# A decoder layer with 32 experts: the last expert pair's rows added by one-hot products on TensorE, and routing weights applied by diagonal products

## The reference

```
g_w, g_idx = top_k(softmax(xt @ w_rg + b_rg), 1)          # one group of 4
e_w, e_idx = top_k(softmax(e_logits of that group), 2)    # two experts of its 8
w = e_w / sum(e_w) * g_w
for e in range(32):
    h = silu(xt @ w_e_gate[e]) * (xt @ w_e_up[e])         # 1024 -> 256
    y = y + combine[:, e:e + 1] * (h @ w_e_down[e])       # 256 -> 1024
x = x + y;  out = rmsnorm(x, final_norm_g)
```

## Time and profile before

| | |
|---|---|
| median of 3 runs | 892.48 us (892.04 to 895.05) |
| the profiled execution's own time | 894.15 us |
| its span, first to last instruction | 892.4 us |
| PE, DVE, ACT, POOL busy | 89%, 42%, 24%, 9% of the span |
| expert weights | 96 transfers of 1 MB |
| mean granted clock of TensorE | 0.965 of full speed |

### The profile page before, as it was taken

The page is one execution under the profiler, slowest core; times in us unless marked ns, Lnnn a source line. Parts: engine busy times, 40 slices in busy tenths (PEclk is TensorE's granted clock), DMA queues, the critical chain, the costliest instruction groups (busy, mean ns, idle before and its releaser), DMA issues. The chain is left out here.

```text
span 892.4 us, 12013 instructions
## 1 busy us (share of the span) xinstructions
PE 795.0 (89%) x4643; PEld 583.0 (65%) x4643; DVE 371.0 (42%) x859; ACT 211.5 (24%) x388; POOL 77.1 (9%) x106
## 2 busy tenths in 40 slices
PE   5999999999999899999899999998999977787730
PEld 4887887779788666679899988987333322332210
DVE  2597566661700467348343347455111111101118
ACT  2320300001242334455343242120111100100003
POOL 0100230000111000000000000012111101001000
PEclk9999999999999999999999999997999999989975
DMA  9461283121446433310214344079999999999846
GB/s 365 158 203 48 72 90 105 52 90 55 172 164 215 166 112 126 142 49 1 95 60 166 142 176 157 25 295 386 380 418 419 420 422 421 419 421 421 338 115 262
DMA packets 33976, 186.09 MB, mean 209 GB/s; under 512 B 5915, under 2 KB 6187, under 8 KB 16808
## 3 DMA queue, kind: packets, MB, share of 16 engines
q1 hardware_dynamic: 21712, 146.63, 41.5%
q0 software_dynamic: 11344, 35.21, 12.4%
q10 hardware_dynamic: 864, 3.47, 1.0%
HBM read 176.14 MB, written 17.22 MB: 217 GB/s over the span
## 5 line engine op out<-in xcount | busy, mean ns | idle before, releaser
L479 PE MATMUL ps<-sb 128*128 128x288 f32 (+14 forms) x3038 | 595.3, 430 | 55.9 <-DMA sb<-in_wexp 32.4
L479 PEld LDWEIGHTS ps<-sb 128*128 128x128 f32 (+5 forms) x3038 | 388.2, 169 | 235.6 <-issue 149.1
L479 PE MATMUL ps<-sr 128*128 128x288 f32 (+1 forms) x1200 | 158.5, 292 | 1.2 <-DVE sr L1767 1.2
L479 PEld LDWEIGHTS ps<-sr 128*128 128x128 f32 x1200 | 155.1, 189 | 2.1 <-DVE sr L1767 1.4
L488 PEld LDWEIGHTS ps<-sb 128*128 128x128 f32 (+3 forms) x405 | 41.7, 140 | 35.4 <-issue 27.9
L2018 DVE SCALAR_TENSOR_TENSOR sb<-sb,ps 128x256 f32<-128x256 f32 x16 | 6.7, 421 | 125.2 <-ACT sb L1352 125.2
L488 PE MATMUL ps<-sb 128*128 128x128 f32 (+3 forms) x405 | 53.4, 270 | 4.9 <-DVEq L1846 2.0
L1767 DVE TENSOR_TENSOR sr<-sb,sr 128x2048 fp32r<-128x2048 f32 (+2 forms) x25 | 45.0, 1818 | 16.0 <-ACT sr L1239 12.8
L2026 DVE COPY sb<-ps 128x1024 f32<-128x1024 f32 x16 | 19.6, 1224 | 75.0 <-PE ps L479 75.0
L1057 ACT ACTIVATE sb<-ps 128x576 f32<-128x576 f32 (+4 forms) x29 | 22.9, 789 | 94.6 <-PE ps L479 66.9
L1755 DVE SCALAR_TENSOR_TENSOR sb<-sb,ps 128x576 f32<-128x576 f32 x24 | 18.0, 752 | 62.3 <-PE ps L479 62.3
(11 more groups left out here) (243 smaller groups left out, 435.8 us busy)
## 6 DMA issues: line engine op xcount, KB each, us to landing
sb<-in_wexp SPq DMA_DIRECT2D x96, 1024.0 KB, 28.8
sb<-in_wstream SPq DMA_DIRECT2D x34, 1024.0 KB, 5.0
sb<-in_mkT POOLq DMA_DIRECT2D x8, 512.0 KB, 7.3
sb<-in_mv POOLq DMA_DIRECT2D x8, 512.0 KB, 5.3
sb<-expert_rows SPq DMA_DIRECT2D x8, 512.0 KB, 9.3
sb<-in_xT ACTq DMA_DIRECT2D x4, 576.0 KB, 8.9
sb<-in_x SPq DMA_DIRECT2D x4, 512.0 KB, 7.3
sb<-k_pad POOLq DMA_DIRECT2D x8, 256.0 KB, 10.4
```

The lines of the kernel that those rows point to most:

```text
L479: return signed(nc.tensor.matmul(*a, **kw))
```

## The change

The diff also merges some semaphores of the first stages into one (`ones_set`, `zero_set`; `exp_ssm`, `trig`; `y_built`, `vt_built`), with the same points waited for. The rest is this:

- **The last pair isn't scattered.** `HELD` is pair 15. Its result stays in `M_YO` in SBUF. Instead of it, at the beginning of the expert stage, POOL scatters a tile of zeros to its rows of `expert_rows` (a memset of 128x1024, and one scatter after the gather of pair 2).
- **One-hot matrices.** In the expert stage, after pairs 9 to 13, DVE builds for each token tile (`hold`) a matrix that has a token's routing weight at the slot of pair 15 that holds it, and two diagonal matrices of the tile's weights w0 and w1. PE turns the one-hot matrices at pair 14 (`turn_held`, five transposes) and ACT copies them (`held_turned`, three copies).
- **The sum on PE.** At the end PE forms for each token tile, in PSUM, diag(w0) * y0 + diag(w1) * y1 + onehot * y15: three products for each half of 512 columns, six for each tile, 30 in all. DVE then adds PSUM to h in one operation.
- **Blocks of the last pair reordered.** `down(14)` stands ahead of `gate_up(15, 1)`, on PE and in the list of chunks, and `result(14)` ahead of `hidden(15)` on DVE.
- **Loads.** The five tiles of `expert_rows` go to ring slots that are free by then, and their loads wait for the scatters of pairs 0 to 14 and of the zeros. The load of the gain stands ahead of them in SP's order, and waits only for the turn of pair 15's rows.

```
@@ plan_chunks
-            chunks += [("gu", i, h, x) for h in range(2) for x in range(2)] if i < end else []
-            chunks += [("d", i - 1, 0, x) for x in range(2)] if i > first else []
+            halves = [[("gu", i, h, x) for x in range(2)] for h in range(2)] if i < end else [[], []]
+            before = [("d", i - 1, 0, x) for x in range(2)] if i > first else []
+            chunks += halves[0] + before + halves[1] if i == end - 1 else halves[0] + halves[1] + before
@@ SP
+            sp.wait_ge(xt_ps, NPAIR)
+            load_gain()
+            sp.wait_ge(ew_used, FIRST_Y + TT)
+            for s in range(2):
+                sp.wait_ge(y_sent[s], 16 * (NPAIR // 2))
+            load_results()
+
             with sp.If(overflow(sp) > 0):
...
-            for s in range(2):
-                sp.wait_ge(y_sent[s], 16 * (NPAIR // 2))
-            sp.dma_start(at(M_GF, (1, D)), bass.AP(rows.tensor, rows.offset + D, [[0, P], [1, D]])).then_inc(ld["gf"], 16)
-            for t in range(TT):
-                R = WROWS[t]
-                for k in range(2):
-                    sp.dma_start(at(A_WG + t * 2048 + k * D, (1, D), pn=R),
-                                 y_d[k * T + WTOK[t]:k * T + WTOK[t] + R, :]).then_inc(ld_row[t], 16)
@@ PE
+            def turn_held():
+
+                pe.wait_ge(pick_ready, 2 * TT)
+                pe.wait_ge(hT_sb, HELD - 1)
+                for t in range(TT):
+                    R = WROWS[t]
+                    last = turn_tile(pat(2, HELD_PS[t], (1, R)), at(R_SEL[t], (1, 128), pn=R), at(O_ID, (1, R), pn=R))
+                last.then_inc(held_ps, 1)
+
             def body(i, first, last):
                 gate_up(i, 0)
                 if not first:
                     turn_hidden(i - 1)
+                if last:
+                    down(i - 1)
                 gate_up(i, 1)
                 if not last:
                     turn_rows(i + 1)
-                if not first:
+                if i == HELD - 1:
+                    turn_held()
+                if not first and not last:
                     down(i - 1)
...
+            pe.wait_ge(held_sb, 1)
+            for t in range(TT):
+                R = WROWS[t]
+                if t == TT - 1:
+                    pe.wait_ge(y_sum, t - 3)
+                pe.wait_ge(ld_row[t], 48 if t < TT - 1 else 64)
+                for k in range(2):
+                    for half in range(2):
+                        mm(pat(t % 4, half * 512, (1, 512), pn=R), at(DIAG_AT[2 * t + k], (1, R), pn=R),
+                           at(Y_AT[t] + k * D + half * 512, (1, 512), pn=R), start=(k == 0), stop=False)
+                if t == 0:
+                    pe.wait_ge(y_copied, NPAIR)
+                for half in range(2):
+                    last = mm(pat(t % 4, half * 512, (1, 512), pn=R), at(R_SEL[t], (1, R)),
+                              at(M_YO + HELD % 2 * 1024 + half * 512, (1, 512)), start=False, stop=True)
+                last.then_inc(more_ps, 1)
@@ ACT
+            def held_turned():
+
+                act.wait_ge(held_ps, 1)
+                fn(at(R_SEL[1], (1, 384)), pat(2, HELD_PS[1], (1, 384)), ACT.Copy)
+                fn(at(R_SEL[4], (1, 128)), pat(2, HELD_PS[4], (1, 128)), ACT.Copy)
+                c.do(fn(at(R_SEL[0], (1, 64)), pat(2, HELD_PS[0], (1, 64)), ACT.Copy), held_sb)
@@ DVE
+            def hold(t):
...
+                for k in range(2):
+                    op(v.tensor_scalar(at(DIAG_AT[2 * t + k], (1, R), pn=R), at(O_ID, (1, R), pn=R),
+                                       at((R_W0, R_W1)[k] + t, (1, 1), pn=R), None, ALU.mult), False)
+                    op(v.tensor_tensor(at((R_SEL[t], tmp)[k], (RB, 2), (1, RB), pn=R), at(R_IOTA, (0, 2), (1, RB), pn=R),
+                                       at(R_RA + n5 * k + t, (0, 2), (0, RB), pn=R), ALU.is_equal))
+                    op(v.tensor_tensor(at((R_SEL[t], tmp)[k], (RB, 2), (1, RB), pn=R), at((R_SEL[t], tmp)[k], (RB, 2), (1, RB), pn=R),
+                                       at(R_HW + 2 * n5 * k + 2 * t, (1, 2), (0, RB), pn=R), ALU.mult))
+                c.do(v.tensor_tensor(at(R_SEL[t], (1, 128), pn=R), at(R_SEL[t], (1, 128), pn=R), at(tmp, (1, 128), pn=R), ALU.add),
+                     pick_ready)
...
             def pairs(i0, i1):
                 for i in range(i0, i1):
+                    if i == i1 - 1:
+                        result(i - 1)
                     hidden(i)
-                    if i > i0:
+                    if i0 < i < i1 - 1:
                         result(i - 1)
+                    if HELD - 6 <= i < HELD - 1:
+                        hold(i - HELD + 6)
                 result(i1 - 1)
...
-                dve.wait_ge(ld_row[t], 48 if t < TT - 1 else 64)
-                op(v.scalar_tensor_tensor(h, at(A_WG + t * 2048, (1, D), pn=R), at(R_W0 + t, (1, 1), pn=R), h, ALU.mult, ALU.add))
-                c.do(v.scalar_tensor_tensor(h, at(A_WG + t * 2048 + D, (1, D), pn=R), at(R_W1 + t, (1, 1), pn=R), h,
-                                            ALU.mult, ALU.add), y_sum)
+                dve.wait_ge(more_ps, t + 1)
+                c.do(v.tensor_tensor(h, h, pat(t % 4, 0, (1, D), pn=R), ALU.add), y_sum)
@@ POOL
+            nc.gpsimd.memset(at(M_YO + HELD % 2 * 1024, (1, 1024)), 0.0).then_inc(xg_clear, 1)
...
+                    if i == 0:
+                        scatter(HELD, zeros=True)
                     if i > i0:
                         scatter(i - 1)
-                scatter(i1 - 1)
```

More of the change, by code:

```diff
@@ L161 @@
 R_BV, R_CNT = R_LG, R_TM
+HELD = NPAIR - 1
+R_HW = R_GE
+HELD_PS = [768, 256, 384, 512, 640]
+DIAG_AT = [R_RH + 128 * j for j in range(4)] + [O_KTS + 128 * j for j in range(4)] + [M_WR + 128 * j for j in range(2)]
+FIRST_Y = CHUNK_AT["gu", HELD - 1, 0, 1] - 4
+Y_AT = [SLOTS_E[(FIRST_Y + t) % NSLOT] for t in range(TT)]
+M_TJ = SLOTS_E[(FIRST_Y + TT + 1) % NSLOT]
 assert 10 * OVER <= 40 * TT
-assert _at[0] <= O_Z
+assert _at[0] <= O_Z and O_KTS + 512 <= O_ID and M_WR + 256 <= M_BR
 def plan_jobs():
@@ L1017, in _ @@
             pairs(0, NPAIR)
-            with pe.If(overflow(pe) > 0):
+            flag = overflow(pe)
+            with pe.If(flag > 0):
                 pe.wait_ge(oh2_ready, 1)
@@ L1026, in _ @@
                 pairs(NPAIR, NPAIR_ALL)
+                pe.wait_ge(y_copied, NPAIR_ALL)
+                for t in range(TT):
+                    pe.wait_ge(ld_row[t], 80 if t < TT - 1 else 96)
+            pe.wait_ge(held_sb, 1)
+            for t in range(TT):
+                R = WROWS[t]
+                if t == TT - 1:
[11 more added lines that the diff above has]
+                last.then_inc(more_ps, 1)
         @block.scalar
@@ L1363, in pairs @@
                         rows_turned(i + 1)
+                    if i == HELD - 1:
+                        held_turned()
                 hidden_turned(i1 - 1)
@@ L1374, in _ @@
                 act.wait_ge(y_sum, t + 1)
-                fn(at(M_JUNK, (1, D), pn=R), at(O_H + t * D, (1, D), pn=R), ACT.Square, accum_out=ss).then_inc(ssf, 1)
+                fn(at(M_TJ, (1, D), pn=R), at(O_H + t * D, (1, D), pn=R), ACT.Square, accum_out=ss).then_inc(ssf, 1)
                 act.wait_ge(ssf, t + 1)
@@ L1513, in _ @@
                 if hf:
-                    c.do(ins, y_built)
+                    c.do(ins, ssm_built)
                 else:
@@ L2053, in _ @@
                 numbers(R_TB, NPAIR, OVER // 2)
+                dve.wait_ge(held_sb, 1)
+                for t in range(TT):
+                    op(v.memset(at(R_SEL[t], (1, 128)), 0.0))
                 pairs(NPAIR, NPAIR_ALL)
+                dve.wait_ge(ld["gf"], 32)
             c = main
@@ L2184, in gather, with scatter @@
                     bounds_check=T - 1, oob_is_err=False).then_inc(xg_ready[i % 2], 16)
-            def scatter(i):
-                pool.wait_ge(y_copied, i + 1)
+            def scatter(i, zeros=False):
+                if zeros:
+                    pool.wait_ge(xg_clear, 2)
+                else:
+                    pool.wait_ge(y_copied, i + 1)
                 pool.indirect_dma_start(
@@ L2199, in pairs @@
                         gather(i + 2)
+                    if i == 0:
+                        scatter(HELD, zeros=True)
                     if i > i0:
                         scatter(i - 1)
-                scatter(i1 - 1)
-                for s in range(2):
-                    pool.wait_ge(y_sent[s], 16 * (i1 // 2))
             pairs(0, NPAIR)
+            for s in range(2):
+                pool.wait_ge(y_sent[s], 16 * (NPAIR // 2))
             with pool.If(overflow(pool) > 0):
                 pool.wait_ge(idx_ready, 3)
+                for t in range(TT):
+                    pool.wait_ge(ld_row[t], 48 if t < TT - 1 else 64)
+                scatter(HELD)
                 pairs(NPAIR, NPAIR_ALL)
+                scatter(NPAIR_ALL - 1)
+                for s in range(2):
+                    pool.wait_ge(y_sent[s], 16 * (NPAIR_ALL // 2 + s))
```

62 lines of the change are left out of this document (39 added, 23 removed).

## The result

| | before | after |
|---|---|---|
| median | 892.48 us (892.04 to 895.29, 5 runs) | 901.02 us (899.33 to 901.58, 5 runs) |
| ratio, 95% interval | | 1.0079 [1.0057, 1.0101] |
| profiled execution, span | 892.4 us | 899.8 us |

The change makes the kernel slower by 0.8% or 7 us by the ratio, which is taken over all runs; the two medians lie 8.5 us apart. The forecast was 893.8 us and no measurable difference. The time lies above the range of 891.2 to 896.8.

What follows compares the result with a forecast made beforehand. Weight stream bounds the kernel up to 846 us, then a serial end. Products start at 860.2, plus 26.1 and a 7.4 us tail make span 893.7, +1.3 us, so median 893.8; range 891.2 to 896.8 us.

Steps and rivals of the forecast that it cites:

- The stream and the free parts: Up to 846 us: weight stream sets the pace; zero scatter, hold, transposes, copies and merged semaphores cost 0, bounds 0 to 1.1 us.
- The last pair: Reordered pair 15: gate_up(15, 1) takes 5.29 us, down(15) starts at 854.85, 1.5 us later than before, and ends at 858.5.
- The start of the products: After down(15): PE ready past its branch at 860.05, first tile's results there at 860.5; start taken as 860.2.
- The products: Serial end on PE: 30 products of 512 columns at 0.871 us each, 5.2 us a tile, 26.1 us in all.
- a granted clock of 0.5 behind 860 us: Sign named in advance that the forecast was wrong: PE at the lower clock level during the final products.
- the mechanism as a rival: PE's clock falls under the final products after idle times: 1.64 us a stretch, 895.4 or 897.1 us; chance 0.22.
- if the results came late: Rival before the products: first tile's results at 862.1 or later, time 895.7 us and more; chance 0.12.
- The tail: From the last product to the span's end: DVE's last sum 1.3 us plus 6.1 us, together 7.4 us.
- From the span to the median: Last step of the sum: span 893.7 against 892.4 is +1.3 us, added to the median 892.48 for 893.8.
- The forecast's own balance: Serial end: products begin 9.3 us before DVE did, but take 26.1 + 1.3 us against 16.8, a cost of 10.6.
- the hidden branch: Rival at the products' start: PE ready at 858.5, results there too, 1.7 us less, 892.1 us; chance 0.13.
- half-price products: Rival in the products: 0.456 us each as in a pair, 13.7 us for 30, time 881.4 us; chance 0.06.

Runs made afterwards that it cites:

- fill at the branch: The changed kernel plus four thrown-away products of 512 columns between down(15) and PE's reading of the overflow number: 896.45 us, 1.0042 to the kernel before.
- no block: The changed kernel with PE's overflow block and its branch left out: 897.32 us, 1.0049 to the kernel before.
- version with both losses mended: The changed kernel with PE's overflow branch taken right behind down(14), plus three thrown-away products behind down(15): 894.07 us, 1.0014 to the kernel before.
- early branch: The changed kernel with PE's overflow flag read and branch taken right behind down(14), the rest of pair 15 in both arms: 896.99 us, 1.0048 to before.
- all but the reorder: The changed kernel with the last pair's blocks in the old order, gate_up(15, 1) then down(14): 902.42 us, 1.0099 to the kernel before.
- first tile last: The changed kernel with the end's token tiles in the order 1, 2, 3, 4, 0, so the 64-row tile comes last: 898.70 us, 1.0069 to before.
- one-hot products only: The changed kernel with only the 10 one-hot products on PE, DVE adding both weighted terms: 890.28 us, 0.9970 to the kernel before.
- one diagonal, one on DVE: The changed kernel with w0 * y0 and the one-hot products on PE (20 products), w1 * y1 on DVE: 887.89 us, 0.9946 to before.

## Why the prediction was wrong

**The stream and the free parts: right.** Weight waits 31.9 us against 32.4. The zero scatter, `hold`, the transposes and the copies together cost no more than the 0.7 us by which the block at 840.58 came later (841.29), and start times differ by more than that from kernel to kernel.

**The last pair: right.** `down(15)` was forecast at 854.85 to 858.5, and it is at 854.85 to 858.50. The whole trace runs 0.7 us later (841.29 for `down(14)`, whose place began at 840.58), and `gate_up(15, 1)` (5.15 us against 5.29) and the hand-overs gave that back, so the hit to the hundredth is luck. So is the 5.29 itself: the wait of 2.4 to 2.5 us for the last weights stands in all twelve traces, and the block behind it ran low in two of them, before and after. In the other ten it took 3.65.

**The start of the products: 1.3 us short.** Forecast 860.2, measured 861.51. The results were better than forecast (859.26 against 860.5), so PE itself was what came late. The step was "I take 5.2 us: PE ready at 854.85 + 5.2 = 860.05": that rests on the duration in one row, 4.17 us, and the branch took 5.56, so that PE was ready 6.5 us behind the start of `down(15)`. In the kernel with the fill at the branch it took 5.60, in the others 3.3 to 4.4 us. A duration that varies that much wanted a range of its own in the sum. By the Trainium skill (Advanced Engine Details and Errata, Control Flow Timing) a compare-and-branch takes some 108 ns. The rows of this branch on PE are 31 to 52 times that, and the measurement decides.

**The products: the step that failed.** The term read "30 of them 26.1 us", at the upper level for all. It measured 30.90, +4.8. At the upper level the same 30 take 26.27 us (no block; fill at the branch), so the duration per product was right and the level was wrong. The sign that the prediction had named, a granted clock of 0.5 behind 860 us, is there. I had the mechanism as a rival, and mis-sized it twice. Its chance was 0.22, though the trace said that 2.49 us of idle time were followed by the lower level and my own sum put 1.7 us of pause there, and 3.6 if the results came late. And its price was 1.64 us a stretch, two at the most, since I took it that the clock comes back at once when PE works without a gap. The row around 605 us, with 64-row products at 0.50 and PE busy for 5.00 of 5.00, spoke against that, and I let it stand as an argument for the trigger only. The first tile has 64 rows, and under nearly the whole of it the clock stayed down, from 861.5 to 870.9; at half the speed that costs half of 9.4 us, 4.7. By the Trainium skill (TensorE: Matmul & The Clock Gate, What's actually happening) the throttled state is the default, and activity releases it. The trace agrees on the fall. The release came too, but late: PE worked without a gap from 861.51 on and was at 1.2 GHz up to about 870.9.

**The tail: right.** 892.41 to 899.8 is 7.4 us, as forecast. So 893.7 + 1.3 + 4.8 = 899.8, the span measured.

**From the span to the median: 1.1 us short.** The forecast of 893.8 missed the median of 901.02 by 7.2 us, and the two steps above are 6.1 of them. The rest is the step by which the 1.3 us over the span of 892.4 were added to the median of 892.48: the execution profiled before had taken 894.15, 1.67 above that median, and the one profiled after took 901.58, 0.56 above its own. Without this the forecast would still have missed.

**The structure: right in size, and underweighted.** The forecast's own balance was a gain of 9.3 us paid with 10.6. The version with both losses mended has 1.0014, +1.3 us. The balance held, and it left no room for anything going wrong: most mishaps were on the slow side. Of the two rivals on the better side, the hidden branch was worth 1.7 us only, and half-price products had a clear row against them. The chances should have leaned further that way.

**Open.** Why PE's branch takes 3.3 us in one kernel and 5.6 in another was not tried. In the two slowest cases it lies beside the loads of the results, but so, nearly, do the 4.0 and 4.4 us ones, and in the kernel before it took 4.17 with no such loads beside it. In two kernels (no block, early branch) single runs range from 894 or 896 to 900 us. That this is the clock falling in some runs and not in others fits the two profiles, but the mean clocks of the runs, which take in the whole span, don't settle it: with the early branch the slowest run (899.97 us, the one profiled) had 0.982 and the fastest (895.80 us) 0.978. Why a pause of 2.4 us brought the clock down in some traces and not in others is open too.

## What to carry to other kernels

When a change puts TensorE work behind a stage in which TensorE had been done, price it at both clock levels, and look in the trace for the tile shape that comes first after the pause: if that shape runs at the lower level elsewhere with PE fully busy, take its whole length at that level as the price. One trace shows one draw of the clock: of a block that ran low behind a wait, don't assume that it will again. A few thrown-away products in the pause are the cheap cure, and a branch past a long block belongs where the engine waits for data anyway. Before moving elementwise work to PE, compare the two engines' times per tile in the serial end, since there the slower one is the path; dividing the work between them gave 0.9946 (0.9925 with the early branch and the fill) where moving all of it gave 1.0079.

## What the hardware did that I had not expected

- Four useless products of about 0.9 us each made the kernel 3.3 us faster by the ratios. They ended 0.35 us before the useful ones, which then ran 26.27 us and not 30.90.
- 64-row products nearly kept the level that they found: in three traces (after, early branch, all but the reorder) the clock stayed low for 9.4 us or more, all or nearly all of the six of the first tile; where it was up when they began, all 30 products took 26.27 us. With 128 rows first it came back after some 6 us (one trace).
- The clock was low under the products where PE had paused for 2.35 us (early branch), 3.00 (after), 3.77 (first tile last) or 6.11 (without the reorder) ahead of them. It wasn't where the pause was 0.35, 0.55, 1.42 (one-hot products only) or 1.83 us (one diagonal, one on DVE). But a wait of 2.43 to 2.51 us for the last weights left the next block at 3.65 us in ten of twelve traces.
- One and the same branch on PE took 3.32, 3.33, 3.37, 3.39, 3.70, 3.96, 4.17, 4.27, 4.44, 5.56 and 5.60 us in the eleven kernels that have it; the second branch of the early version, which is not taken, took 0.08 us.
